# Doubling levels of a 64x64 triangular inverse: 32 of 64 columns a head instead of all

## The chip, the cores and the metric

The kernel runs on one core of one Trainium2 chip. The metric is the device time of one launch in microseconds (us). Before the change three runs gave 3709.69, 3712.32 and 3714.06 us, so the median is 3712.32 us. Lower is better. Engine names as in the profile: PE is the matmul engine (TensorE), PEld its weight loads, DVE the vector engine, ACT the scalar engine, POOL GpSimd, SP the queue that starts most transfers.

## The reference, cut to what matters

A model of four layers on 512 tokens of width 1024, in fp32: two layers of a first kind, then two of a second kind (`l` = 0 and 1 below). A layer of the second kind has three mixers side by side: an attention over picked keys (DSA), the RWKV-7 recurrence and the gated delta rule. The last two are recurrences over time with 4 heads of width 64 each. In chunks of 64 tokens the delta rule reads:

```python
lower = jnp.where(strict, jnp.einsum('bhncd,bhnsd->bhncs', kb, k) * decay, 0.0)
sol = lax.linalg.triangular_solve(jnp.eye(C) + lower, rhs,      # C = 64
                                  left_side=True, lower=True, unit_diagonal=True)
u, wk = sol[..., :Dv], sol[..., Dv:]
```

RWKV-7 is given as a step-by-step scan, and has a chunked form of the same kind. So for each chunk of 64 tokens and each of 8 heads a unit triangular 64x64 matrix has to be inverted or solved with. That inverse is the place of the change.

## The kernel before, in words

Each engine has its own program, and semaphores tie them together. The 512 tokens are four tiles of 128. A tile holds two chunks of 64 tokens: chunk 0 in partitions 0 to 63, chunk 1 in partitions 64 to 127. The function `rec_tile(l, j, stock)` stands once in the program of each of PE, DVE, ACT and POOL and handles tile `j` of layer `l` for both recurrences: 4 RWKV heads in columns 0 to 255 and 4 delta-rule heads in columns 256 to 511, 64 columns a head. It is a generator: each `yield` ends a step, and `tile_rounds` (L417) puts the steps of neighbouring tiles in turn, so that the instructions of tile `j`'s inverse stand in each engine's queue between the preparation of tile `j+1` and the end of tile `j-1`. The order on each engine is fixed by this at build time. Tile 0's preparation and most of its inverse lie in the rounds of the DSA attention (`mixer_rounds`, L370). The other three tiles come after it, with only the recurrence to do, and behind them the output projection begins.

The inverse is built by doubling. `Dm` starts as the identity plus level 0, `Dt` is its transpose, `N` the strictly triangular matrix (negated). Level k = 1 to 5 joins blocks of width 2^k into blocks of twice that:

- PE: `Y_k = N^T-product with Dm` (each head and chunk one 64x64 by 64x64 matmul), in two groups `g` of four heads, one PSUM bank a group, keys `("y", k, g)`. It waits for `Dm` of the level before.
- ACT (L3309): copies each group, 128x256, from the bank to `Yk` in SBUF. Key `("Y", k, g)`.
- PE: `d_k` from `Dt` and `Yk` into one bank of 512 columns; it waits for both copies and for `Dt` of the level before. For k < 5 also `dt_k` from `Yk` and `Dt`, the transposed product.
- DVE (L2617): copies `d_k` into `Dm` with a predicate, 128x512, where the mask of level k is 1; for k < 5 (L2623) the same for `dt_k` into `Dt`.

The masks `lvm(k, tr)` (L636) hold a 64x64 pattern that is broadcast over the heads: for `tr` = 0 it is 1 only in columns whose block of width 2^k has an odd number (and rows of the even block beside it), for `tr` = 1 only in columns of even blocks. All other columns are computed and never copied, or copied to `Yk` and used only for columns that no mask keeps.

The helper `each` (L1595 to L1601, its matmul L1600) issues 8 matmuls a group: 4 heads by 2 chunks, the two chunks in different halves of the array's rows and columns. In the trace a matmul of fp32 operands is two instructions. Per tile and layer that is 10 groups for Y, 10 for d, 8 for dt, 16 instructions each; for 4 tiles and 2 layers 3584 instructions, 80 copies on ACT, 40 on DVE at L2617 and 32 at L2623.

`keep_warm(b, n)` (L752) issues n matmuls of 384 columns whose result is not used. Before the change three such places stand in the recurrence (12 of them in tile 1, L1501, and 12 in tile 3 at level 1, L1609, and some between attention units). They stay as they are.

Of the kernel before, what the change touches and what calls it, by code (L numbers as in the profile page):

```python
# [9 lines left out]
I32 = mybir.dt.int32  # L10
# [5 lines left out]
P = 128  # L16
T = 512
NT = 4
D = 1024
# [424 lines left out]
def build_program(nc, A, out, dbg):  # L444
    ctx = ExitStack()
    with ctx:
# [54 lines left out]
        def bc(ap, shape):  # L501
            return ap.broadcast_to(shape)
# [7 lines left out]
        def h64(ap, n):  # L510
            return ap.rearrange("p (h d) -> p h d", h=n)
# [39 lines left out]
        rows, o = {}, 0  # L551
# [81 lines left out]
        def c64(n, k=1):  # L633
            return cr[:, R_X + n * 64:R_X + (n + k) * 64].bitcast(F32)

        def lvm(k, tr, n=4):  # L636
            return bc(c64(k + 6 * tr).unsqueeze(1), [P, n, 64])

        mc_bibs, mc_br, mc_id = c64(12, 2), c64(14), c64(15)
        HALF = (slice(0, 64), slice(64, 128))  # L640
# [81 lines left out]
        def tensor_program(pe):  # L722
# [26 lines left out]
            mm = partial(pe.matmul, skip_group_check=True)  # L749
            tr = partial(pe.transpose, identity=ident)  # L750
# [685 lines left out]
            def rec_tile(l, j, stock):  # L1436
# [8 lines left out]
                def S(*k):  # L1445
                    return pe.sig("rec", *k, l, j)
# [5 lines left out]
                for n, srcs in enumerate(([hbT[:, a, js] for a in range(4)],  # L1452
                                          [hbT[:, 4, js], hbT[:, 5, js], gT[:, 4, js], gT[:, 5, js]],
                                          [gT[:, a, js] for a in range(4)])):
                    b, free = bank(K("in", n), K("in", n))
                    pe.wait_ge(*free)
                    for m, s in enumerate(srcs):
                        ins = tr(b[:, m * P:(m + 1) * P], s)
# [8 lines left out]
                ins = mm(b1[:, 0:256], hbT[0:32, 6, js], lora[0:32, :], True, True)  # L1467
                if l:
                    pe.wait_ge(*at("rec", "vz", l))
                    ins = mm(b1[:, 256:512], vz[0:32, js], vup[0:32, :], True, True)  # L1470
# [18 lines left out]
                for p in range(4):  # L1489
                    ins = mm(b3[:, 256 + 2 * p:258 + 2 * p], LW[:, p * P:(p + 1) * P], ind, True, True)  # L1490
# [8 lines left out]
                b, free = bank(K("F4"), K("F4"), of=("rec", "od", l, j - 2) if j > 1 else None)  # L1499
# [3 lines left out]
                for a in range(2):  # L1503
                    tr(b[:, (2 * a + 0) * P:(2 * a + 1) * P], QK[:, a * P:(a + 1) * P])
                    ins = tr(b[:, (2 * a + 1) * P:(2 * a + 2) * P], KB[:, 256 + a * P:384 + a * P])
# [5 lines left out]
                b, free = bank(K("F3"), K("F3"), of=("rec", "o", 0, l, j - 2) if j > 1 else None)  # L1511
                pe.wait_ge(*free)
                pe.wait_ge(*at(*K("Qh")))
                for a in range(2):
                    tr(b[:, a * P:(a + 1) * P], QK[:, 256 + a * P:384 + a * P])
                    ins = tr(b[:, (2 + a) * P:(3 + a) * P], Qh[:, 256 + a * P:384 + a * P])
# [3 lines left out]
                b, free = bank(K("F1"), K("F1"))  # L1520
                pe.wait_ge(*free)
                pe.wait_ge(*at(*K("KBx")))
                for a in range(2):
                    tr(b[:, (2 * a) * P:(2 * a + 1) * P], Qh[:, a * P:(a + 1) * P])
                    ins = tr(b[:, (2 * a + 1) * P:(2 * a + 2) * P], KB[:, a * P:(a + 1) * P])
# [5 lines left out]
                b, free = bank(K("F2"), K("F2"))  # L1531
                pe.wait_ge(*free)
                pe.wait_ge(*at(*K("BT")))
                for a in range(4):
                    ins = tr(b[:, a * P:(a + 1) * P], BT[:, a * P:(a + 1) * P])
# [3 lines left out]
                b, free = bank(K("gd"), K("DN0"))  # L1539
                pe.wait_ge(*free)  # L1540
                pe.wait_ge(*at("rec", "gg", l))
                for h in range(4):
                    for c in HALF:
                        ins = mm(b[c, h * 64:(h + 1) * 64], bc(gg[c, j, h:h + 1], [64, 64]), m_bi[c, c], True, True)
# [4 lines left out]
                for par in range(2):  # L1549
                    if par:  # L1550
                        yield
                    b, free = bank(K("RW", par), K("RW", par))
# [4 lines left out]
                    for q in range(2):  # L1557
                        for n in range(2):
                            for e_, c in enumerate(HALF):
                                o = q * 256 + n * P  # L1560
                                ins = mm(b[c, o:o + P].rearrange("p (c n) -> p c n", c=2),
                                         F2[rs, n * 256 + q * P + 64 * e_:n * 256 + q * P + 64 * e_ + 64],
                                         f1v[rs, q, :, c], True, True)
                    ins.then_inc(*S("rw", par))
                yield
                N = get()
                for par in range(2):
                    b, free = bank(K("N", par), K("N", par))
# [4 lines left out]
                    for a, (lhs, rhs) in enumerate(((f1v, F2), (f4v, F3))):  # L1573
                        for q in range(2):
                            for e_, c in enumerate(HALF):
                                ins = mm(b[c, (2 * a + q) * 64:(2 * a + q + 1) * 64], lhs[rs, q, 1, c],
                                         rhs[rs, q * P + 64 * e_:q * P + 64 * e_ + 64], True, True)
                    ins.then_inc(*S("n", par))
                yield
                for par in range(2):  # L1580
                    b, free = bank(K("PN", par), K("PN", par))
                    pe.wait_ge(*free)
                    rs = HALF[par]
                    for q in range(2):
                        for e_, c in enumerate(HALF):
                            ins = mm(b[c, q * P:(q + 1) * P].rearrange("p (c n) -> p c n", c=2),
                                     F3[rs, q * P + 64 * e_:q * P + 64 * e_ + 64], f4v[rs, q, :, c], True, True)
# [3 lines left out]
                PN, Dm, Dt = get(), get(), get()  # L1591
                yield MADE
                stock.put(pe, l, DTN, F4)

                def each(b, g, lhs, rhs, o=0):  # L1595

                    for h in range(4):
                        for c in HALF:
                            hs = slice(g * 256 + h * 64, g * 256 + h * 64 + 64)
                            ins = mm(b[c, o + h * 64:o + (h + 1) * 64], lhs[c, hs], rhs[c, hs], True, True)  # L1600
                    return ins  # L1601

                yield
                for k in range(1, 6):
                    Yk = get()
                    for g in range(2):
                        b, free = bank(K("y", k, g), K("Y", k, g))
                        pe.wait_ge(*free)
                        keep_warm(b, 12 if j == 3 and k == 1 and not g else 0)  # L1609
                        pe.wait_ge(*at(*K("D", k - 1, g)))  # L1610
                        each(b, g, N, Dm).then_inc(*S("y", k, g))
                    if j == 3 and k == 4:
                        for q in ("dve", "act"):
                            pe.wait_ge(*at("dsa over", l, q))
                        to_T(("out", l), mx, lambda i, c: ("rec", "mixed", l, i), (0,))
                    yield
                    b, free = bank(K("d", k), K("D", k, 1), of=K("y", k, 0))
                    pe.wait_ge(*free)
                    pe.wait_ge(*at(*K("Dt", k - 1)))
                    for g in range(2):  # L1620
                        pe.wait_ge(*at(*K("Y", k, g)))
                        ins = each(b, g, Dt, Yk, 256 * g)
                    ins.then_inc(*S("d", k))
                    if k < 5:
                        b, free = bank(K("dt", k), K("Dt", k), of=K("y", k, 1))
                        pe.wait_ge(*free)
                        for g in range(2):
                            ins = each(b, g, Yk, Dt, 256 * g)
                        ins.then_inc(*S("dt", k))
                    if j == 3 and k == 4:  # L1630
                        to_T(("out", l), mx, lambda i, c: ("rec", "mixed", l, i), (1,))
                    stock.put(pe, l, Yk)
                    yield
# [3 lines left out]
                b, free = bank(K("x"), K("X"))  # L1637
# [4 lines left out]
                for h in range(4):  # L1642
                    o = (h // 2) * 256 + 192
                    for c in HALF:
                        ins = mm(b[c, h * 64:(h + 1) * 64], RW[h % 2][c, o:o + 64], VV[c, h * 64:(h + 1) * 64], True, True)
                ins.then_inc(*S("x"))
                for e_, c in enumerate(HALF):
                    b, free = bank(K("wt", e_), K("WT", e_))
# [10 lines left out]
                for par in range(2):  # L1659
# [4 lines left out]
                    for q in range(4):  # L1664
                        h = 2 * q + par
# [115 lines left out]
        def vector_program(v):  # L1781
# [19 lines left out]
            def psum_of(*key):  # L1801
                return psum[book.bank.get(key, 0)]
# [673 lines left out]
            def rec_tile(l, j, stock):  # L2476
                js = slice(j * P, (j + 1) * P)

                def K(*k):
                    return ("rec",) + k + (l, j)  # L2480

                def S(*k):
                    return v.sig("rec", *k, l, j)
# [126 lines left out]
                for k in range(1, 6):  # L2610
                    Yk = get()
                    if j == 3 and k == 5:
                        low(("out", l), 0)
                    yield
                    v.wait_ge(*at(*K("D", k - 1, 1)))
                    v.wait_ge(*at(*K("d", k)))
                    v.copy_predicated(h64(Dm, 8), lvm(k, 0, 8).bitcast(I32),  # L2617
                                      h64(psum_of(*K("d", k))[:, :], 8)).then_inc(*S("D", k, 1))
                    v.also(*K("D", k, 0))
                    if k < 5:  # L2620
                        v.wait_ge(*at(*K("Dt", k - 1)))
                        v.wait_ge(*at(*K("dt", k)))
                        v.copy_predicated(h64(Dt, 8), lvm(k, 1, 8).bitcast(I32),  # L2623
                                          h64(psum_of(*K("dt", k))[:, :], 8)).then_inc(*S("Dt", k))
                    stock.put(v, l, Yk)
                    if j == 3 and k == 5:
                        low(("out", l), 1)
                    yield
# [113 lines left out]
        def scalar_program(s):  # L2742
# [38 lines left out]
            def psum_of(*key):  # L2781
                return psum[book.bank.get(key, 0)]
# [427 lines left out]
            def rec_tile(l, j, stock):  # L3210
                def K(*k):
                    return ("rec",) + k + (l, j)

                def S(*k):
                    return s.sig("rec", *k, l, j)
# [89 lines left out]
                for k in range(1, 6):  # L3305
                    Yk = get()
                    for g in range(2):
                        s.wait_ge(*at(*K("y", k, g)))
                        copy(Yk[:, g * 256:g * 256 + 256], psum_of(*K("y", k, g))[:, 0:256]).then_inc(*S("Y", k, g))  # L3309
                    yield  # L3310
                    stock.put(s, l, Yk)
                    if j == 3 and k > 3:
                        high(("out", l), k - 4)
                    yield
# [479 lines left out]
```

## Time and profile before

| | |
|---|---|
| Median of 3 runs | 3712.32 us (3709.69 to 3714.06) |
| Profiled execution | span 3708.2 us; no other time of that execution is given |
| PE busy | 3610.1 us, 97% of the span, 23122 instructions |
| Weight loads (PEld) | 2996.1 us, 81% |
| DVE, ACT, POOL | 1972.4, 1502.7, 1623.7 us |
| Chain that ended last | PE 83%, DVE 10%, ACT 4% |

The busy time of PE is a union over pipelined matmuls: each matmul of 64 columns is recorded with 218 ns, while 64 of them follow each other within about 2 us. So the pace of PE is read from how many instructions fit in a stretch, not from the duration of one. The recurrence of layer l = 0 lies at about 1980 to 2125 us, that of l = 1 at about 3146 to 3296 us.

### The profile page before, as it was taken

To read this page: it belongs to the slowest core of one execution; us is meant where nothing else is said; L and a number is where in the kernel's file an instruction comes from. 1 tells how busy PE (TensorE), PEld (TensorE's weight loads), DVE (VectorE), ACT (ScalarE), POOL (GpSimd) and SP (SyncE) were. 2 spreads that over 40 slices of the span, in tenths; PEclk is the share of its full clock that TensorE was granted. 3 is DMA by queue.
4 is the path that set the end of the run, shared out by engine and by line. 5 is a ranking of instruction groups with operands and counts; after the bars stand their busy time and mean duration, and the time that the engine had idled before them with its cause. 6 is when DMAs were issued, how large, how long until landed. Compare 5 with 4: busy or idle time off the path is not lost.

```text
span 3708.2 us, 55795 instructions
## 1 busy us (share of the span) xinstructions
PE 3610.1 (97%) x23122; PEld 2996.1 (81%) x23122; DVE 1972.4 (53%) x3453; ACT 1502.7 (41%) x2665; POOL 1623.7 (44%) x883
## 2 busy tenths in 40 slices
PE   9999999999899999999999899999999999999999
PEld 8878888888788888888767888888888866788887
DVE  2356554344645544553677745544652496765552
ACT  3444333434433343333555443334333455534332
POOL 3114566421266635664322135664665322225664
PEclk9999999999999999999999999999999999999999
DMA  4103332311243234322210034323332220012332
GB/s 130 40 29 99 112 103 68 89 52 35 69 136 102 63 101 132 103 63 89 74 46 2 3 125 121 103 66 112 103 102 81 83 57 24 3 42 89 99 103 97
DMA packets 393405, 291.95 MB, mean 79 GB/s; under 512 B 17056, under 2 KB 355904, under 8 KB 393152
## 3 DMA queue, kind: packets, MB, share of 16 engines
q1 hardware_dynamic: 387728, 284.49, 25.2%
q10 hardware_dynamic: 5136, 2.70, 0.4%
q8 instruction: 183, 3.00, 0.3%
q0 software_dynamic: 288, 1.18, 0.1%
q14 instruction: 70, 0.57, 0.1%
HBM read 286.24 MB, written 2.10 MB: 78 GB/s over the span
## 4 chain that ended last, share of the span: by engine, by line
PE 83%; DVE 10%; ACT 4%; issue 1%; POOL 1%; ACTq 0%; DMA 0%; DVEq 0%; SPq 0%; POOLq 0%
PE ps L811 13%; PE ps L812 13%; PE ps L813 13%; PE ps L1040 4%; PE ps L1042 4%; PE ps L1041 4%; PE ps L943 3%; PE ps L940 3%; PE ps L942 3%; PE ps L1068 2%; PE ps L1600 2%; PE ps L1088 2%; PE ps L1077 1%; PE ps L1150 1%; PE ps L838 1%
## 5 line engine op out<-in xcount | busy, mean ns | idle before, releaser
L3453 POOL TENSOR_TENSOR wl<-wraw,wh 128x1024 fp32r<-128x1024 f32 (+1 forms) x424 | 1026.4, 2426 | 1553.1 <-ACT wh L2771 1549.6
L811 PE MATMUL ps<-x_T,wh 128*128 128x512 f32 (+1 forms) x2224 | 850.2, 382 | 0.0
L812 PE MATMUL ps<-x_T,wh 128*128 128x512 f32 (+1 forms) x2224 | 849.0, 382 | 0.0
L813 PE MATMUL ps<-x_T,wl 128*128 128x512 f32 (+1 forms) x2224 | 849.0, 382 | 0.0
L2771 ACT ACTIVATE wh<-wraw 128x1024 fp32r<-128x1024 f32 (+1 forms) x424 | 446.0, 1053 | 763.1 <-PE ps L813 489.1
L811 PEld LDWEIGHTS ps<-x_T,wh 128*128 128x128 f32 x2224 | 418.5, 188 | 81.1 <-issue 0.5
L813 PEld LDWEIGHTS ps<-x_T,wl 128*128 128x128 f32 x2224 | 418.4, 188 | 80.6
L812 PEld LDWEIGHTS ps<-x_T,wh 128*128 128x128 f32 x2224 | 418.4, 188 | 80.7 <-issue 0.5
L2048 DVE TENSOR_TENSOR scr<-scr,ps 128x512 f32<-128x512 f32 x132 | 90.7, 687 | 465.3 <-ACT scr L2926 465.3
L1040 PE MATMUL ps<-wh,h_T 128*128 128x512 f32 x672 | 262.5, 391 | 0.4
L1041 PE MATMUL ps<-wl,h_T 128*128 128x512 f32 x672 | 261.5, 389 | 0.0
L1042 PE MATMUL ps<-wh,h_T 128*128 128x512 f32 x672 | 261.5, 389 | 0.0
L3449 POOL TENSOR_TENSOR wl<-arena,wh 128x512 fp32r<-128x512 f32 x126 | 187.7, 1493 | 121.9 <-ACT wh L2768 121.8
L2094 DVE SCALAR_TENSOR_TENSOR x_tm<-ps,x_tm 128x512 f32<-128x512 f32 x224 | 155.0, 692 | 157.6 <-PE ps L943 78.3
L3449 POOL TENSOR_TENSOR wl<-mix,wh 128x512 fp32r<-128x512 f32 x150 | 212.6, 1433 | 8.2 <-ACT wh L2768 8.2
L2055 DVE TENSOR_TENSOR scr<-scr,ps 128x512 f32<-128x512 f32 x96 | 65.9, 686 | 217.4 <-PE ps L813 216.8
L1040 PEld LDWEIGHTS ps<-wh,h_T 128*128 128x128 f32 x672 | 126.1, 188 | 30.4 <-POOL wl L3449 2.7
L1042 PEld LDWEIGHTS ps<-wh,h_T 128*128 128x128 f32 x672 | 126.1, 188 | 26.3
L1041 PEld LDWEIGHTS ps<-wl,h_T 128*128 128x128 f32 x672 | 126.1, 188 | 25.8
L2768 ACT ACTIVATE wh<-mix 128x512 fp32r<-128x512 f32 x150 | 91.8, 624 | 125.3 <-PE ps L813 47.8
L940 PE MATMUL ps<-wh,h_T 128*128 128x512 f32 x352 | 138.0, 392 | 0.0
L943 PE MATMUL ps<-wh,h_T 128*128 128x512 f32 x352 | 137.1, 390 | 0.0
(816 smaller groups left out, 6877.6 us busy)
## 6 DMA issues: line engine op xcount, KB each, us to landing
wraw<-in_ffn_w_gate_dram SPq DMA_DIRECT2D x88, 512.0 KB, 3.9
wraw<-in_ffn_w_up_dram SPq DMA_DIRECT2D x88, 512.0 KB, 3.9
wraw<-in_w_in_dram SPq DMA_DIRECT2D x82, 512.0 KB, 3.8
wraw<-in_w_gate_dram SPq DMA_DIRECT2D x44, 512.0 KB, 3.9
wraw<-in_w_up_dram SPq DMA_DIRECT2D x44, 512.0 KB, 3.8
mix<-in_ffn_w_down_dram SPq DMA_DIRECT2D x20, 1024.0 KB, 7.1
arena<-in_ffn_w_down_dram SPq DMA_DIRECT2D x12, 1024.0 KB, 6.2
wraw<-in_ffn_w_down_dram SPq DMA_DIRECT2D x24, 512.0 KB, 3.7
```

Source lines behind the costliest of these rows:

```text
L811: mm(b[:, t0:t1], wh[:, k, :], xTh[:, k, t0:t1], k == 0, False)
L812: mm(b[:, t0:t1], wh[:, k, :], xTl[:, k, t0:t1], False, False)
L813: ins = mm(b[:, t0:t1], wl[:, k, :], xTh[:, k, t0:t1], False, k == 7)
L940: mm(o, lh(k, j), wh[:, q, :], k == 0, False)
L943: ins = mm(o, ll(k, j), wh[:, q, :], False, k == K - 1 and not apart)
L1040: mm(b[:, :], hF[:, q, 0, m, t], wh[:, u, :], first and q == 0, False)
L1041: mm(b[:, :], hF[:, q, 0, m, t], wl[:, u, :], False, False)
L1042: ins = mm(b[:, :], hF[:, q, 1, m, t], wh[:, u, :], False, q == pairs - 1)
L2094: return stt(xs, b[:, :], -0.5 if minus else 0.5, xs, ALU.mult, ALU.add)
L2771: copy(hl_of(w)[0], raw_of(w)).then_inc(*s.sig("w", "hi", w))
L3449: tt(wl[:, u, :], fast_src(prod, q), wh[:, u, :].bitcast(F32), ALU.subtract).then_inc(*g.sig("w", "lo", w, u))
L3453: tt(wl, raw_of(w), wh.bitcast(F32), ALU.subtract).then_inc(*g.sig("w", "lo", w))
```

## The change

The matmuls of levels 1 to 5 stream 32 of the 64 columns of their moving operand: the odd blocks of `Dm` for Y, the odd blocks of `Yk` for d, the even blocks of `Dt` for dt. The results lie side by side ("packed") in the bank, 32 columns a head: 128 columns a group, 256 for all. The stationary operand keeps its 64 columns, and the number of matmuls stays. ACT copies 128 packed columns a group into the odd blocks of `Yk` and leaves the even blocks with what the buffer held. DVE copies 256 packed columns with a predicate into the odd blocks of `Dm` (even blocks of `Dt`), with the mask cut to the same columns. Waits, keys, banks, buffers and the order of instructions on each engine stay.

```diff
+        def level(ap, k, odd):
+            return ap.rearrange("p (b s n) -> p b s n", s=2, n=2 ** k)[:, :, odd, :]
+        def packed(ap, k):
+            return ap.rearrange("p (b n) -> p b n", n=2 ** k)
+        def heads_of(ap, k):
+            return ap.rearrange("p (h b) n -> p h b n", h=8)
+        def level_mask(k, tr):
+            m = level(c64(k + 6 * tr), k, 1 - tr)
+            return bc(m.unsqueeze(1), [P, 8, 32 // 2 ** k, 2 ** k]).bitcast(I32)
...
-                            ins = mm(b[c, o + h * 64:o + (h + 1) * 64], lhs[c, hs], rhs[c, hs], True, True)
+                            ins = mm(packed(b[c, o + h * 32:o + (h + 1) * 32], k), lhs[c, hs], level(rhs[c, hs], k, odd),
+                                     True, True)
...
-                        each(b, g, N, Dm).then_inc(*S("y", k, g))
+                        each(b, g, k, N, Dm, 1).then_inc(*S("y", k, g))
...
-                        ins = each(b, g, Dt, Yk, 256 * g)
+                        ins = each(b, g, k, Dt, Yk, 1, 128 * g)
...
-                            ins = each(b, g, Yk, Dt, 256 * g)
+                            ins = each(b, g, k, Yk, Dt, 0, 128 * g)
...
-                    v.copy_predicated(h64(Dm, 8), lvm(k, 0, 8).bitcast(I32),
-                                      h64(psum_of(*K("d", k))[:, :], 8)).then_inc(*S("D", k, 1))
+                    v.copy_predicated(heads_of(level(Dm, k, 1), k), level_mask(k, 0),
+                                      heads_of(packed(psum_of(*K("d", k))[:, 0:256], k), k)).then_inc(*S("D", k, 1))
...
-                        v.copy_predicated(h64(Dt, 8), lvm(k, 1, 8).bitcast(I32),
-                                          h64(psum_of(*K("dt", k))[:, :], 8)).then_inc(*S("Dt", k))
+                        v.copy_predicated(heads_of(level(Dt, k, 0), k), level_mask(k, 1),
+                                          heads_of(packed(psum_of(*K("dt", k))[:, 0:256], k), k)).then_inc(*S("Dt", k))
...
-                        copy(Yk[:, g * 256:g * 256 + 256], psum_of(*K("y", k, g))[:, 0:256]).then_inc(*S("Y", k, g))
+                        copy(level(Yk[:, g * 256:g * 256 + 256], k, 1),
+                             packed(psum_of(*K("y", k, g))[:, 0:128], k)).then_inc(*S("Y", k, g))
```

## Rows read from the trace of the kernel before

**Rows 1.** The page: the chain that ended last, shares of the span by engine.

```profile
PE 83%; DVE 10%; ACT 4%; issue 1%; POOL 1%; ACTq 0%; DMA 0%; DVEq 0%; SPq 0%; POOLq 0%
```

**Rows 2.** Ten windows that cover both recurrences: sum of lengths, busy us by engine.

```profile
sum 295.00, PE 266.97 PEld 235.97 DVE 225.21 ACT 136.70 POOL 57.67; mean PE 26.70 PEld 23.60 DVE 22.52 ACT 13.67 POOL 5.77
```

**Rows 3.** The same ten windows, L1600 alone.

```profile
sum 295.00, PE 128.98 PEld 118.01; mean PE 12.90 PEld 11.80
```

**Rows 4.** Chain of waits, layer 0, tile 1 in order: start, us, what.

```profile
2027.82 0.73 DVE arena L2623
...
2044.22 0.74 DVE scr L2617
...
2054.84 0.59 issue
```

**Rows 5.** Chain of waits, layer 1, tiles 0, 1 and 3.

```profile
3172.26 0.64 DVE spare L2617
...
3213.10 0.58 issue
...
3283.89 0.74 DVE wraw L2617
```

**Rows 6.** Groups by form on DVE and ACT: busy, mean ns.

```profile
L2617 DVE COPY_PREDICATED scr<-cr,ps 128x512 f32<-128x512 int32 x5 | 3.7, 736 | 1.2 <-PE ps L1600 1.2
...
L2607 DVE COPY_PREDICATED scr<-cr,spare 128x256 f32<-128x256 int32 x1 | 0.4, 443 | 0.0
...
L3179 ACT ACTIVATE scr<-ps 128x256 f32<-128x256 f32 x8 | 3.1, 384 | 7.3 <-PE ps L1077 7.2
...
L3179 ACT ACTIVATE scr<-ps 128x384 f32<-128x384 f32 x5 | 2.5, 491 | 1.9 <-PE ps L1077 1.8
```

**Rows 7.** Timeline of PE, runs of equal matmuls: start, us, form, idle before.

```profile
2035.16 0.95 PE L1490 MATMUL ps<-con,spare 128*128 128x2 f32 x8
...
2055.19 0.60 PE L1586 MATMUL ps<-scr 64*64 64x128 f32 x12
2055.73 1.53 PE L1458 MATMUL ps<-cr,arena 128*128 128x128 f32 x12
...
3219.11 1.08 PE L1600 MATMUL ps<-scr,spare 64*64 64x64 f32 x29 [0.17 <-DVE scr L2617]
```

**Rows 8.** Timeline of PE around a fall of the clock in the first layer.

```profile
720.57 2.73 PE L1334 MATMUL ps<-con,arena 128*128 128x1 f32 x24
...
724.58 0.63 PE L813 MATMUL ps<-x_T,wl 128*128 128x512 f32 x1
```

**Rows 9.** Windows: length, busy PE, PEld, DVE, ACT, POOL, granted clock, DMA.

```profile
724.10:727.50 3.40, 3.40 (x9) 2.65 (x9) 0.36 (x4) 2.16 (x2) 1.15 (x1) 0.51 0.21 72
...
2038.00:2042.00 4.00, 3.99 (x132) 3.79 (x126) 3.76 (x9) 3.31 (x12) 0.00 (x0) 1.00 0.02 4
2042.00:2045.00 3.00, 0.94 (x7) 0.50 (x5) 2.86 (x9) 0.74 (x2) 1.97 (x2) 1.00 0.00 0
2045.10:2048.10 3.00, 3.00 (x38) 2.55 (x39) 2.93 (x5) 1.26 (x3) 2.64 (x3) 0.50 0.00 0
...
3213.30:3216.50 3.20, 2.55 (x64) 2.29 (x66) 3.13 (x5) 1.85 (x4) 2.84 (x3) 1.00 0.02 5
...
3229.60:3232.90 3.30, 3.30 (x43) 2.65 (x43) 1.42 (x4) 0.38 (x1) 0.00 (x0) 0.50 0.01 2
```

**Rows 10.** Chain of waits: the same work at either clock, layer 1 tiles 1 and 2.

```profile
3192.09 1.01 PE ps L1667 x29
3194.14 1.63 PE ps L1600 x56
...
3230.80 1.79 PE ps L1667 x29
3234.46 2.53 PE ps L1600 x56
```

**Rows 11.** Share of L1600 in the chain of waits of layer 0's recurrence.

```profile
by line: PE ps L1600 28.2%; issue 4.8%; PE ps L1686 2.8%; PE ps L1667 2.3%; PE ps L1561 1.8%; PE ps L1088 1.7%; POOL small L3495 1.6%; PE ps L1484 1.5%; DVE small L2664 1.5%; PE ps L1696 1.5%; PE ps L781 1.5%; DVE spare L2579 1.4%; PE ps L1
```

More of the change, by code:

```diff
@@ L1593, in rec_tile, with each @@
                 stock.put(pe, l, DTN, F4)
-                def each(b, g, lhs, rhs, o=0):
+                def each(b, g, k, lhs, rhs, odd, o=0):
                     for h in range(4):
```

## The prediction

> **What bounds the kernel.** I read the page's chain first: PE holds 83% of it, DVE 10% [rows 1]. Outside the two recurrences nothing changes, so I went on to windows over those stretches. They are 295 us long in all; PE is busy for 267.0 of them, DVE for 225.2, ACT for 136.7 [rows 2]. The changed matmuls (L1600) make up 129.0 us of PE's busy time, and their weight loads are busy for 118.0 [rows 3]. So neither engine sets the pace alone: the chain changes between them several times a tile. The reader should look in it for two things: copies at L2617 and L2623 that stand on it, and stretches of L1600. In layer 0's recurrence L1600 holds 28.2% of the chain [rows 11].
>
> **Part 1: the copies.** Today a predicated copy of 512 columns takes 736 ns, one of 256 columns 443 ns [rows 6]: -0.29 us a copy. There are 72 of them (40 at L2617, 32 at L2623), so DVE loses 21 us of work. Most of that stands beside other work. On the chain of layer 0 I count for tile 1: L2623 at 2027.82 (DVE goes on to L2645, for which PE waits), L2617 at 2044.22 (PE waits for it), and L2617 before the "issue" piece at 2054.84, where DVE can begin its next product only after the copy [rows 4]. Tile 2 repeats the pattern, tile 3 has two (after its wait for tile 2's end, and at level 5). That is 8, or -2.3 us. Layer 1: two in tile 0 (3172.26 and the L2623 behind it), then in tiles 1 and 2 the same three, L2623 at 3213.10 in addition, and one at level 4 of which only 0.17 us can be had, since PE waits no longer than that [rows 5, 7]; two in tile 3 (the first at 3283.89) [rows 5]. That is 2 + 2 x 4 + 2 = 12, plus 2 x 0.17: -3.8 us. ACT's copies shrink by 0.11 us each (384 ns for 256 columns, 491 for 384, so half of 256 saves 491 - 384 = 107) [rows 6]; 80 copies make 8.6 us, nearly all beside PE; about two are on the path: -0.2 us. Sum of part 1: -6.3 us.
>
> No row shows a copy whose pieces are only 2 elements long with gaps of 2, as at level 1. Bounds: 0 if the gaps eat the saving everywhere, -0.29 as taken; the same count of copies with 0 saved gives 0. Below, if DVE were the pace for all 21 us and ACT hidden: -21. I take -6.3, since the packed side and most levels have long pieces.
>
> **Part 2: what PE's instructions cost.** The number stays (3584), the weights stay 64 columns, the streamed columns halve. What paces a matmul, weights or streamed columns? With weights of 128 columns, 8 matmuls of 2 columns take 0.95 us and 12 of 128 columns take 1.53 us; take off the last one's tail (0.2) and it is 0.11 and 0.12 us each, for 64 times the columns [rows 7]. So there the weight load sets the pace. With weights of 64 columns, 29 L1600 take 1.08 us, 0.031 each, and 12 L1586 with 128 columns take 0.54 us from their start to that of the next group, 0.045 each [rows 7]. If the columns entered linearly, 32 fewer would save (0.045 - 0.031)/2 = 0.007 us each, 25 us in all, about half of it on the path (28.2% of the 140 us of layer 0 are 39.5 [rows 11], and L1600 has half of its 129 us [rows 3] there). Bounds: 0 and -13 us. I take 0, because of the 2-column row. PE's reads of `Dm` and `Yk` now have gaps; a read even twice as slow would fit under the load, so I take 0 here too.
>
> **Part 3: the clock.** This is where I expect the change to cost. PE runs at 2.4 GHz except in some stretches, and in the first layer one fall comes with no idle at all: 24 matmuls of one column, back to back for 2.73 us, and soon after them 512-column matmuls of 0.63 us [rows 8] at a granted clock of 0.51, that is 1.2 GHz [rows 9]. PE was full of instructions, but streamed almost nothing. In the recurrence: a window dense with L1600 (132 matmuls in 4 us) runs at 1.00; 3 us in which PE did only 7 transposes are followed by 0.50 [rows 9]; and the start of tile 2's levels in layer 1 (from 3229.60), after a wait of PE and one group of L1600, runs at 0.50 too [rows 9]. Against it: the same transposes before 3213.30 in layer 1 were followed by 1.00 [rows 9]. So the recurrence already runs near the point where the clock falls, and the change takes half the streamed columns out of its commonest matmul. It also makes it harder to come back: after a fall, the matmuls that should lift the clock stream half as much.
>
> Price: L1667 x29 takes 1.79 us at the lower clock and 1.01 at the full one, L1600 x56 2.53 (the last of it at full clock) and 1.63 [rows 10]. So 1.68 us are lost in 4.32, or 0.39 us for each us at 1.2 GHz. Today 13.5 us of the recurrences run there (two stretches of 3.4 in layer 0, one of 6.7 in layer 1, found by moving such windows along; [rows 9] show a part of one of each kind): 5.3 us paid already. Places a layer where thin work meets L1600: tile 0's levels between attention units; the first level of tiles 1 and 2 (as at 3227); the transposes amid tiles 1 and 2, and the wait in tile 3. I count five a layer, the two first levels as one, ten in all, and leave out one, in layer 1, where DVE sets the pace (L2623 at 3213.10 on the chain [rows 5]) and would hide it. Nine falls of 6.8 us (as the one from 3229.60) at 0.39 are 23.9 us; less the 5.3 paid today: +18.6. This is the least certain term: bounds 0 (the clock doesn't see the difference) and half of the 295 us at the lower clock, 57.5 - 5.3 = +52.
>
> The Trainium skill, "TensorE: Matmul & The Clock Gate", section "Why this matters for your kernels", says that drops mid-kernel come from long idle gaps of PE between bursts. By that rule the changed levels, still dense, would keep the clock, and the sum would be that of rival 1 below. The trace disagrees at 720.57, where there was no gap [rows 8].
>
> **Sum.** -6.3 + 0 + 18.6 = +12.3 us. The profiled execution has a span of 3708.2 us, 4.1 below the median of the runs, 3712.3; I apply the difference to the median: 3724.6 us (+0.33%).
>
> **Rivals.**
> 1. The clock stays as it is, the copies pay. For it: no tile's L1600 run fell by itself, and the 3213.30 row. Against it: rows 8. Time: 3712.3 - 6.3 = 3706.
> 2. The other side, by PE: columns set part of L1600's pace. Then -13 - 6.3 = -19, 3693. For it: L1586's 0.045 against 0.031; against it the 2-column row. It decides if a 32-column matmul follows the last within 0.027 us instead of 0.031.
> 3. A few more falls: three of 6.8 us beyond those paid, 8.0 - 6.3 = +2, 3714.
> 4. The change doesn't save what it says: the gapped copies take as long as before, with the falls: +18.6, 3731; without them, 3712.
>
> **Chances.** Forecast 0.46, rival 1 0.28, rival 3 0.13, rival 2 0.07, rival 4 0.06. A difference under 0.2% (7.4 us) can't be told from none here. Rival 1 lies just inside of it, and I give it a third of its chance beyond: with rival 2, faster is 0.17. Same: the rest of rival 1, rival 3 and a part of the forecast, 0.36. Slower: 0.47. Range: from rival 1, a little below, 3704, to 3750, where +44 of part 3's upper bound of +52 would be reached.
>
> **What would show it.** L2617 and L2623 at about 440 ns, L3309 at about 280 (part 1); L1600 still at 0.031 us each at full clock (part 2); a granted clock under 1.00 in far more of 1980 to 2125 and 3146 to 3296 us, above all in tile 0's levels and in tile 3 (part 3). I am wrong if those windows show the same 13.5 us at 0.50 as today, or if L1600's pace at full clock falls under 0.028 us.

## The result, and the profile after

The changed kernel takes 3762.0 us (median of 4 runs, 3760.12 to 3767.52) against 3711.0 us of the kernel before (4 runs, 3707.47 to 3714.06): ratio 1.0136, 95% interval 1.0124 to 1.0148. It is 51 us slower. The forecast was 3724.6 us with a range to 3750; the direction was right, the size four times too small.

In what follows a thin matmul is one that streams 32 columns. In the diffs and rows below, L1615 is the matmul that was L1600, L2633 and L2639 are the predicated copies that were L2617 and L2623, and L3325 is ACT's copy that was L3309.

The page after: the 40 slices of PE and of the clock it was granted, and the chain by engine, which answers to [rows 1].

```profile
span 3761.5 us, 55795 instructions
...
PE   9999999999999999999999999999999999999999
...
PEclk9999999999999999999997799999999998879999
...
PE 85%; DVE 9%; ACT 4%; issue 1%; POOL 1%; DMA 0%; ACTq 0%; DVEq 0%; SPq 0%; POOLq 0%
```

All slices are full of PE work, and the clock digit falls in slices 22, 23 and 34 to 36: the two recurrences. Before, every digit of that line was 9. The other engines are busy for no longer than before (DVE 1958.8 us against 1972.4, ACT 1495.6 against 1502.7).

The recurrences as windows, from the first level matmul to the last copy, first of the kernel before, then after (columns as in [rows 9]: length, busy us of PE, PEld, DVE, ACT, POOL, granted clock).

```profile
1984.00:2121.00 137.00, 125.90 (x3008) 112.04 (x3008) 104.37 (x232) 64.11 (x157) 28.93 (x24) 0.98 0.01 3
3150.00:3292.00 142.00, 127.83 (x3014) 113.72 (x3014) 108.89 (x240) 64.35 (x157) 28.75 (x24) 0.98 0.01 3
```

```profile
1985.00:2146.00 161.00, 151.97 (x3008) 137.74 (x3008) 98.28 (x232) 60.98 (x158) 28.72 (x24) 0.78 0.01 3
3179.60:3344.00 164.40, 154.25 (x3014) 140.06 (x3014) 102.10 (x240) 61.42 (x157) 28.57 (x24) 0.77 0.01 2
1986.00:2010.00 24.00, 24.00 (x308) 21.63 (x304) 5.37 (x19) 6.38 (x22) 0.00 (x0) 0.51 0.01 2
2054.30:2074.80 20.50, 19.96 (x280) 18.44 (x280) 13.85 (x30) 7.01 (x14) 5.69 (x5) 0.51 0.01 2
2098.70:2115.80 17.10, 16.66 (x272) 15.62 (x272) 10.70 (x21) 4.55 (x11) 4.86 (x5) 0.51 0.01 2
2136.20:2149.90 13.70, 13.16 (x195) 12.18 (x194) 7.80 (x17) 3.88 (x9) 0.00 (x0) 0.51 0.01 1
3180.70:3204.60 23.90, 23.90 (x299) 21.52 (x297) 5.05 (x17) 6.54 (x23) 0.00 (x0) 0.50 0.01 1
3252.40:3269.50 17.10, 16.24 (x250) 15.08 (x247) 10.58 (x21) 5.97 (x13) 3.44 (x3) 0.51 0.01 2
3293.40:3313.90 20.50, 19.76 (x317) 18.51 (x318) 13.83 (x29) 5.63 (x14) 5.89 (x5) 0.50 0.01 2
3330.90:3348.00 17.10, 16.11 (x228) 15.07 (x229) 8.74 (x19) 4.43 (x11) 1.64 (x1) 0.51 0.01 2
```

The same instructions fill 325.4 us instead of 279.0: 46.4 of the 53.3 us between the two spans. PE is busy for 306.2 us instead of 253.7, DVE and ACT for less. The lower eight rows are the stretches at 1.2 GHz, found by moving windows along: four a layer, one for each tile, 13.7 to 24 us long, 154 us in sum. Before there were short ones ([rows 9] show a part of two). In the first of them PE was busy for 24.00 of 24.00 us: nothing waited there, it had only gone slow. All eight begin beside a short pause of PE: 0.63 us ahead of tile 0's levels, 1.65 to 1.69 us amid the transposes of tiles 1 and 2, 1.29 us in tile 3. The kernel before has such pauses at the same places (0.64 us at 1983.96, for one, and no fall behind it), so the pauses alone are not the cause.

The same place in tile 0 of layer 0 on PE's timeline (start, us, form), before and then after:

```profile
1986.86 2.08 PE L1600 MATMUL ps<-spare 64*64 64x64 f32 x64
1988.87 0.66 PE L1088 MATMUL ps<-arena,scr 128*128 128x64 f32 x4
...
1994.17 3.25 PE L1600 MATMUL ps<-spare 64*64 64x64 f32 x96
1997.35 1.53 PE L1458 MATMUL ps<-cr,arena 128*128 128x128 f32 x12
```

```profile
1989.08 3.62 PE L1615 MATMUL ps<-spare 64*64 64x32 f32 x64
1992.64 1.11 PE L1103 MATMUL ps<-arena,scr 128*128 128x64 f32 x4
...
2002.03 5.33 PE L1615 MATMUL ps<-spare 64*64 64x32 f32 x96
2007.29 2.82 PE L1473 MATMUL ps<-cr,arena 128*128 128x128 f32 x12
...
2011.33 0.89 PE L1615 MATMUL ps<-spare 64*64 64x32 f32 x24
```

64 matmuls of half the columns take 3.62 us instead of 2.08. Neighbours that the change doesn't touch slow down with them (L1088, now L1103: 0.66 to 1.11). The full pace is back only behind L1473, twelve matmuls of 128 columns: then 24 of L1615 take 0.89 us. That these wider matmuls lifted the clock is not shown: in the run with tile 0 alone thin, below, they did not.

### The profile page after: what moved, and what is told of

It reads as the page before. It is cut to its first block, busy times and chain, and to the rows that moved or that the text cites. A ratio compares the mean times of both kernels' runs of the same rounds, so it can differ in the third digit from the quotient of the medians.

```text
span 3761.5 us, 55795 instructions
## 1 busy us (share of the span) xinstructions
PE 3670.7 (98%) x23122; PEld 3055.8 (81%) x23122; DVE 1958.8 (52%) x3453; ACT 1495.6 (40%) x2665; POOL 1622.7 (43%) x883
## 4 chain that ended last, share of the span: by engine, by line
PE 85%; DVE 9%; ACT 4%; issue 1%; POOL 1%; DMA 0%; ACTq 0%; DVEq 0%; SPq 0%; POOLq 0%
PE ps L826 13%; PE ps L828 13%; PE ps L827 13%; PE ps L1055 4%; PE ps L1056 4%; PE ps L1057 4%; PE ps L1615 3%; PE ps L958 3%; PE ps L955 3%; PE ps L957 3%; PE ps L1083 2%; PE ps L1103 2%; PE ps L1092 1%; PE ps L1165 1%; PE ps L853 1%
```

## The experiments

Theory: the thinner matmuls make the clock fall in the recurrences and then do not lift it. Rivals: the gapped or packed addresses of the copies or of PE's reads and writes cost the time; or a wait that the new copies bring.

**PE streams all 64 columns, the copies stay short**, from their places in the bank:

```diff
-  ins = mm(packed(b[c, o + h * 32:o + (h + 1) * 32], k), lhs[c, hs], level(rhs[c, hs], k, odd), True, True)
+  ins = mm(b[c, 2 * o + h * 64:2 * o + (h + 1) * 64], lhs[c, hs], rhs[c, hs], True, True)
...
-  heads_of(packed(psum_of(*K("d", k))[:, 0:256], k), k)      # dt and ACT's y likewise
+  heads_of(level(psum_of(*K("d", k)), k, 1), k)
```

> PE streams all 64 columns as before; only the copies on ACT and DVE take the 32 kept columns of each head, straight from their places in the bank. Theory (the clock falls because half as many columns are streamed): the granted clock in both recurrences is as before, about 17 us at 1.2 GHz, and the shorter copies are all that is left: 20 copies on the path at 0.23 us (the 500 ns that the changed kernel shows against 733) and a little of ACT, -5 us against before, 3706. Rival A (the shorter copies move the order of waits and so bring the clock down): 3750 or more. Rival B (gapped reads of the bank cost as much as they save): 3711.

Measured: 3706.9 us against 3713.3, ratio 0.9986 (0.9977 to 0.9995). The windows of its recurrences:

```profile
1986.50:2121.00 134.50, 122.63 (x3008) 109.73 (x3008) 97.62 (x233) 59.77 (x157) 28.72 (x24) 1.00 0.01 3
3150.00:3289.00 139.00, 126.58 (x3014) 113.17 (x3014) 102.19 (x243) 60.67 (x158) 28.57 (x24) 0.98 0.01 3
```

The short copies alone are a small gain (273.5 us for the recurrences, 5.5 under the kernel before), so the loss of the changed kernel must come with the halved matmul. Rival A is out.

**All 64 columns streamed, but in gapped order, kept blocks first**, so that PE reads `Dm`, `Dt` and `Yk` with gaps and the bank holds the kept columns packed:

```diff
-  ins = mm(b[c, 2 * o + h * 64:2 * o + (h + 1) * 64], lhs[c, hs], rhs[c, hs], True, True)
+  ins = mm(halves(b[c, 2 * o + h * 64:2 * o + (h + 1) * 64], k), lhs[c, hs], both(rhs[c, hs], k, odd), True, True)
+  # both: blocks "p (b s n) -> p s b n", the kept s first; halves: "p (s b n) -> p s b n"
```

> PE streams 64 columns a matmul, but in another order: first the 32 kept ones in the same pieces with gaps as in the changed kernel, then the other 32; the copies read the first 32 of each head. Theory (number of columns): clock as before, time as with all 64 in plain order, about 3706. Rival C (the gaps in what PE reads bring the clock down or slow PE, not the number of columns): as the changed kernel, 3750 to 3762.

Measured: 3707.1 us, 0.9983 (0.9974 to 0.9992), the same as the one above. Gaps in PE's operand cost nothing that can be measured here, and the copy gains nothing from a packed source. Only the number of columns streamed is left.

**PE halved, copies whole, nothing packed:**

```diff
+  ins = mm(level(b[c, 2 * o + h * 64:2 * o + (h + 1) * 64], k, odd), lhs[c, hs], level(rhs[c, hs], k, odd), True, True)
   # the copies of the kernel before; what they copy beside the kept columns is not used
```

> PE streams the 32 columns only and writes them to their places in the bank; ACT and DVE copy all 64 columns as before (the other 32 of the bank are what it held, and no mask keeps them). Theory (columns): the falls of the clock stay, the saving of the copies goes: the changed kernel plus 5 us, 3767; about 160 us of both recurrences at 1.2 GHz. Rival A (copies are the cause): 3711.

Measured: 3773.8 us, 1.0160 (1.0146 to 1.0174). Its windows:

```profile
1986.00:2151.00 165.00, 155.67 (x3008) 140.40 (x3008) 105.03 (x232) 64.83 (x157) 28.91 (x24) 0.76 0.01 3
3184.00:3352.00 168.00, 160.50 (x3014) 144.95 (x3014) 109.13 (x240) 65.73 (x157) 28.74 (x24) 0.74 0.01 2
```

The halved matmul by itself is the slowdown, and more than all of it: 60.5 us. Against the kernel before, nothing differs but which columns PE streams.

**The same in tile 0 alone, and in tiles 1 to 3 alone** (`if j == 0`, or `if j > 0`, ahead of the halved `mm`):

> As the run with half stream and full copies, but only in tile 0 of each layer; the other three tiles stream 64 columns. Theory (columns, locally): the long stretch at 1.2 GHz in tile 0's levels, 23.9 us in the changed kernel, comes back in both layers, and the others (tiles 1 to 3) stay as before: 2 x 24 us at 0.39 us lost a us, +19 us at most, 3725; less if tile 0's stretch also moves where later falls land. Rival D (one fall starts the next, so that later tiles fall too): 3740 or more.

> The complement of the run with half stream in tile 0 only: tile 0 streams 64 columns, tiles 1 to 3 the kept 32, copies as before. If each tile's levels bring their own fall, the two parts add up to the run with half stream everywhere (+60.5 us): +60.5 - 23.6 = +37, 3750. If falls chain from tile to tile (rival D), the parts add up to more than the whole: 3755 or over.

Measured: tile 0 alone 3736.9 us, 1.0061 (1.0048 to 1.0075), that is 23.6 us; tiles 1 to 3 alone 3755.4 us, 1.0111 (1.0092 to 1.0129), 41.8 us. Together 65 us, and all tiles at once cost 60.5. Both runs came out above their forecasts (3725 at most, and 3750), and the second lies on the line drawn for rival D, 3755. The sum alone doesn't decide: it is 5 us over the whole, and the two intervals reach 5 and 7 us to either side. The windows do. First those of the run with tile 0 alone thin, two for each layer:

```profile
1986.00:2023.60 37.60, 37.60 (x435) 31.58 (x434) 13.68 (x36) 14.46 (x37) 3.67 (x3) 0.50 0.01 2
2023.60:2137.00 113.40, 103.86 (x2575) 94.20 (x2574) 90.70 (x197) 50.09 (x120) 25.06 (x22) 0.97 0.01 3
3169.00:3194.40 25.40, 25.15 (x328) 22.77 (x329) 7.61 (x21) 7.45 (x23) 0.00 (x0) 0.53 0.00 1
3194.40:3321.70 127.30, 116.64 (x2690) 103.42 (x2686) 101.58 (x221) 57.54 (x135) 28.72 (x24) 0.93 0.01 3
```

Then tile 0's levels, and the first stretch of tile 1, in the run with tiles 1 to 3 thin:

```profile
1986.00:2010.00 24.00, 22.41 (x398) 18.81 (x392) 15.00 (x32) 13.85 (x36) 6.59 (x6) 1.00 0.01 3
2040.70:2057.80 17.10, 17.10 (x267) 15.98 (x265) 11.19 (x21) 6.29 (x12) 3.67 (x4) 0.51 0.01 2
```

A long stretch at 1.2 GHz comes in the tiles that are thin and in no other: tile 0 with 64 columns keeps 1.00, and tile 1 falls though tile 0 had not. So none is only the late return from an earlier fall. Where tile 0 alone is thin, only short falls come behind its stretch: two of 3.4 us in layer 0, as in the kernel before, and 17 us in three pieces in layer 1, where the kernel before has one of 6.7.

The length is less orderly. In layer 1 tile 0's stretch is 24 us in both kernels, but in layer 0 it lasts 37.6 us here against 24 with all tiles thin, though the same work stands in it. PE's timeline of this run:

```profile
2008.44 2.82 PE L1473 MATMUL ps<-cr,arena 128*128 128x128 f32 x12
2018.75 2.07 PE L1499 MATMUL ps<-arena,con 128*128 128x512 f32 x2
```

The twelve matmuls of 128 columns behind which the changed kernel had its full pace back stand here at the same place, run at 1.2 GHz too (2.82 us in both), and the clock stayed down for 12 us more, through four matmuls of 512 columns. What ends a stretch is not shown by these runs.

**Half of the heads thin**, heads 0 and 2 with 32 columns, 1 and 3 with 64, short copies:

```diff
+  if h % 2 == 0:
+      ins = mm(level(b[...], k, odd), lhs[c, hs], level(rhs[c, hs], k, odd), True, True)
+  else:
+      ins = mm(b[...], lhs[c, hs], rhs[c, hs], True, True)
```

> Full-stream kernel with the short copies, but of the four heads of a group the first and third stream their 32 kept columns and the others all 64: 48 on average. Theory (columns): between 3707 (all 64) and 3762 (all 32) with a granted clock between theirs; if the time at 1.2 GHz grows evenly with the columns left out, some 90 us of both recurrences and 3734. If the fall is a matter of crossing a point, far from the middle: under 3715 or over 3750. Rival A or C (something else than the columns): no ordering between the three is forced.

Measured: 3717.2 us, 1.0018 (1.0006 to 1.0031), with runs from 3710 to 3729 us. Its profile is of one near the upper end (span 3727.5): clock 0.95 in layer 0 and 0.86 in layer 1.

```profile
1991.00:2131.00 140.00, 128.33 (x3008) 114.81 (x3008) 98.31 (x234) 60.24 (x157) 28.74 (x24) 0.95 0.01 3
3157.50:3311.40 153.90, 142.84 (x3014) 127.78 (x3014) 101.83 (x240) 60.66 (x157) 28.59 (x24) 0.86 0.01 3
```

The loss goes with how thin the stream is, but not in proportion: halfway in columns is 10 us above all 64 (3706.9) and 45 under all 32 (3762.0), and varies from run to run. It lies between the two outcomes that were named, 3734 for an even growth and under 3715 for a point that is crossed, so the form of the dependence stays open.

**The changed kernel with more work for PE**: two matmuls of 384 columns, of which nobody uses the result, ahead of the first Y group and ahead of d of each level (156 in all).

```diff
-                        keep_warm(b, 12 if j == 3 and k == 1 and not g else 0)
+                        keep_warm(b, 12 if j == 3 and k == 1 and not g else 0 if g else 2)
...
                     pe.wait_ge(*free)
+                    keep_warm(b, 2)
                     pe.wait_ge(*at(*K("Dt", k - 1)))
```

> The changed kernel, with work added: before the first group of Y and before d of each level two matmuls of 128 rows and 384 columns whose result is not used, 160 in all and 0.17 to 0.2 us each (27 to 32 us of PE, some of it inside PE's waits). Theory (the clock answers to streamed columns): the long falls go, 57 us come back, 10 to 30 are paid: 3715 to 3735, faster than the changed kernel although it does more. Rival (the clock falls for another cause in the changed matmuls): the falls stay and the time rises to 3780 or more.

Measured: 3734.8 us, 1.0066 (1.0041 to 1.0091) of the kernel before, and so 27 us less than the changed kernel, which does less work. The runs range from 3729 to 3753 us; these windows are of one that took 3730.5:

```profile
1987.00:2134.00 147.00, 143.21 (x3085) 122.13 (x3084) 97.92 (x232) 60.36 (x157) 28.75 (x24) 1.00 0.01 3
3164.50:3313.00 148.50, 144.31 (x3090) 123.18 (x3090) 101.86 (x240) 61.00 (x157) 28.61 (x24) 1.00 0.01 3
```

The group of those wide matmuls, 294 before and 450 here (busy us, mean ns):

```profile
L770 PE MATMUL ps<-cr 128*128 128x384 f32 x450 | 107.1, 362 | 0.9 <-DVE small L2565 0.9
```

And the same place in tile 0 of layer 0 as above, on PE's timeline:

```profile
1989.99 0.62 PE L770 MATMUL ps<-cr 128*128 128x384 f32 x2
1990.54 2.06 PE L1615 MATMUL ps<-spare 64*64 64x32 f32 x64
1992.53 0.66 PE L1103 MATMUL ps<-arena,scr 128*128 128x64 f32 x4
```

With them the clock stays at 1.00, and 64 thin matmuls take 2.06 us: what 64 of 64 columns took (2.08). That takes the fall away and leaves the change in place. The added matmuls also fill pauses of PE (the one of 0.63 us ahead of tile 0's levels is gone), so this run by itself doesn't tell columns from pauses; the runs above do, with the same pauses and 64 columns. The recurrences last 295.5 us, 29.9 less than in the changed kernel. They are 22.0 above the kernel that streams all 64 columns, which is what the added matmuls cost: too much to be worth it.

**The form of the copy.** The new predicated copies average 491 to 503 ns, not 443 as forecast. By level, in tile 1 of the changed kernel (DVE's timeline, levels 1 and 2):

```profile
2037.94 0.73 DVE L2633 COPY_PREDICATED scr<-cr,ps 128x256 f32<-128x256 int32 x1 [0.26 <-PE ps L1615]
2038.88 0.73 DVE L2639 COPY_PREDICATED arena<-cr,ps 128x256 f32<-128x256 int32 x1 [0.20 <-PE ps L1615]
2043.06 0.43 DVE L2633 COPY_PREDICATED scr<-cr,ps 128x256 f32<-128x256 int32 x1 [0.17 <-PE ps L1615]
```

At level 1, where the kept runs are 2 elements long, the copy of 256 columns takes as long as one of 512 did [rows 6]. Which operand does it? The kernel before, with 32 instructions on 256 columns added at the end of DVE's program (the small helpers that form the patterns are left out; the comments give the line and the operands):

```diff
+ for _ in range(4):                                                                            # line, dst / mask / src
+     step(v.copy_predicated(h8(gap(dst, 2)), m8(gap(mk, 2)), h8(row(src[:, 0:256], 2))))        # 2755 gaps / gaps / packed
+     step(v.copy_predicated(h8(gap(dst, 2)), m8(row(mk[:, 0:32], 2)), h8(row(src[:, 0:256], 2)))) # 2756 gaps / packed / packed
+     step(v.copy_predicated(h8(row(dst[:, 0:256], 2)), m8(gap(mk, 2)), h8(row(src[:, 0:256], 2)))) # 2757 packed / gaps / packed
+     step(v.copy_predicated(h8(row(dst[:, 0:256], 2)), m8(row(mk[:, 0:32], 2)), h8(gap(src, 2)))) # 2758 packed / packed / gaps
+     step(v.copy_predicated(h8(gap(dst, 4)), m8(gap(mk, 4)), h8(row(src[:, 0:256], 4))))        # 2759 runs of 4
+     step(v.copy_predicated(h8(row(dst[:, 0:256], 2)), m8(row(mk[:, 0:32], 2)), h8(row(src[:, 0:256], 2)))) # 2760 packed
+     step(v.tensor_copy(gap(dst, 2), row(src[:, 0:256], 2)))                                    # 2761
+     step(v.tensor_copy(dst[:, 0:256], src[:, 0:256]))                                          # 2762
```

> The kernel before, with 32 instructions added at the end of VectorE's program (four rounds of eight, each of 256 columns, one waiting for the last); what they write is read by nobody. In this order: (1) a predicated copy whose destination and mask are runs of 2 elements with gaps of 2, from a packed source; (2) destination with gaps, mask packed; (3) destination packed, mask with gaps; (4) source with gaps, the other two packed; (5) destination and mask in runs of 4 with gaps of 4; (6) all packed; (7) a plain copy into runs of 2 with gaps; (8) a plain packed copy. The question is which operand makes the level-1 copy of 256 columns take 730 ns where those of levels 2 to 5 take 427 to 444. [...] Rival A: the mask's short runs: (1), (3) near 730, (2) near 430. Rival B: either alone is enough: (1), (2), (3) near 730. Rival C: it is the number of runs in any operand, the source's too: (4) also near 730. If (1) itself is near 430 here, the form of the copy is not the cause at all. Of the time of the whole kernel I expect 15 to 25 us more (32 instructions of 0.4 to 0.75 us), if VectorE ends near the kernel's end.

Measured, groups by form (busy us, mean ns of one):

```profile
L2755 DVE COPY_PREDICATED scr<-cr,ps 128x256 f32<-128x256 int32 x4 | 2.9, 722 | 0.1
L2756 DVE COPY_PREDICATED scr<-cr,ps 128x256 f32<-128x256 int32 x4 | 2.9, 722 | 0.1
L2758 DVE COPY_PREDICATED scr<-cr,ps 128x256 f32<-128x256 int32 x4 | 1.8, 440 | 0.1
L2757 DVE COPY_PREDICATED scr<-cr,ps 128x256 f32<-128x256 int32 x4 | 1.8, 440 | 0.1
L2760 DVE COPY_PREDICATED scr<-cr,ps 128x256 f32<-128x256 int32 x4 | 1.8, 440 | 0.1
L2759 DVE COPY_PREDICATED scr<-cr,ps 128x256 f32<-128x256 int32 x4 | 1.7, 425 | 0.1
L2761 DVE COPY scr<-ps 128x256 f32<-128x256 f32 x4 | 1.7, 425 | 0.1
L2762 DVE COPY scr<-ps 128x256 f32<-128x256 f32 x4 | 1.7, 424 | 0.1
```

It is the destination alone: 722 ns with gaps of 2 in it, 440 with gaps in the mask or the source only, 425 with runs of 4. A plain copy into the same gapped destination takes 425, no more than the packed one (that it would take more was expected, and wrong). What is slow is a predicated copy into runs of 2 elements. The kernel as a whole took 3729.2 us against 3708.1 in its one run, 21 more; its added instructions stand behind each other from 3709.66 to the end.

## Why the prediction was wrong in size

**Part 1, the copies: right in kind, and less than forecast.** The bound of gaps that eat the saving was true at level 1 only: the saving is 0.31 us at levels 2 to 5 and 0 at level 1, 0.24 on average instead of 0.29. ACT's term was right: 384 less 107 was forecast, and it takes 277 ns.

```profile
L3325 ACT ACTIVATE spare<-ps 128x128 f32<-128x128 f32 x36 | 9.8, 277 | 48.0 <-PE ps L1615 47.8
```

The kernel with short copies alone shows the sum: -5.5 us in its recurrences and a ratio of 0.9986, -5.2 us with an interval of -8.5 to -1.9, against -6.3. A part of that is the clock too: layer 0 shows 1.00 there against 0.98 before, so the copies' own share is below 5.5. An estimate: its recurrences have 6.8 us at 1.2 GHz where those of the kernel before have 13.5, and 6.7 us less at the price of 0.37 found below are 2.5 of the 5.5. That leaves about 3 us for the copies, half of the 6.3 forecast; one profile of each kernel is little to rest it on.

**Part 2, PE's pace: right.** At full clock the chain after has

```profile
3274.37 1.01 PE ps L1683 x29
3276.42 1.61 PE ps L1615 x56
```

against 1.63 for 56 of L1600 in [rows 10], beside 29 of the untouched L1667 (now L1683) at 1.01 in both. At 1.2 GHz it is the same: 32 thin matmuls take 1.92 us (at 1994.11 in the changed kernel), 32 of all 64 columns 1.97 (at 2045.09 in the kernel before). Half the columns save nothing. That it is the weights which set the pace was argued from [rows 7]; no run changes them alone. The condition given for rival 2, 0.027 us, doesn't fit its term either: 0.007 us less than 0.031 would be 0.024.

**Part 3, the clock: the mechanism was right, the term mis-sized.** The step that failed is "Nine falls of 6.8 us ... at 0.39". The price held: from the kernel with short copies to the changed one the recurrences grow from 273.5 to 325.4 us, 51.9. The stretches are 154 us in sum; 7.9 of them lie behind the two windows, and the former kernel still has 6.8, so it is for 139 us, 0.37 us for each. The count held roughly: eight stretches instead of nine, at the places that were named, save the first levels of tiles 1 and 2. The length did not: 13.7 to 24 us, 19 on average, where 6.8 was assumed. I took the length from 3229.60, a fall in the kernel before, where the levels behind it still streamed 64 columns. The prediction itself had said that the matmuls which should lift the clock would stream half as much, and then gave that no price. In the changed kernel the levels did not lift it; it stayed down through 256 of L1615 in tile 0 of layer 0, 64, 32, 64 and 96 with attention products between. Why a stretch ends after 14 us in one tile and after 24 in another stays open, as said for the run with tile 0 alone. With 19 in place of 6.8, the prediction's own sum is 8 x 19 x 0.39 = 59 less 5.3 paid and less 6.3 for part 1: +48, against 51 measured. The stated upper bound, half of the 295 us, was about what came, and a chance beyond +44 should have been kept inside the range.

Outside the recurrences' windows the changed kernel's span is 6.9 us longer: 4.6 of it between the two recurrences (1033.6 us against 1029.0) with PE's busy time longer by 6.0, the rest ahead of and behind them. Part of it is the clock too: the 7.9 us of the last stretches, 3.9 of them in that gap. A stretch of 6.8 us at 3153.6, also in the gap, has none beside it in the kernel before, but the kernels with 64 streamed columns show one there as well and are not slower, so it can't be laid to the change.

**The rule on gaps.** The prediction set a fall with no gap at 720.57 against the rule on idle gaps in "TensorE: Matmul & The Clock Gate" of the Trainium skill, section "Why this matters for your kernels". The first stretch of the changed kernel decides: PE busy for 24.00 of 24.00 us at 0.51, and ahead of it a pause of 0.63 us, as long as the one at the same place in the kernel before (0.64 us), where the clock stayed at 1.00. By the rule the time would have been that of rival 1, 3706.

**Rivals.** 1 (the clock stays, 3706) is what the two kernels with 64 streamed columns gave, 3706.9 and 3707.1: its price was right, its condition was not met. 3 (a few falls) is met by none at 32 columns; half of the heads thin comes near it, 3717. 4 (gapped copies take as long as before) is true at level 1 alone, 16 of the 72 copies. 2 is refuted above.

## What to carry to other kernels

Before you cut the columns of small matmuls, ask what their pace is: if the columns don't set it (here 64 matmuls take 2.06 us with 32 columns and 2.08 with 64), the cut saves nothing, and here it held PE at 1.2 instead of 2.4 GHz for 154 us, where 13.5 were before. Don't take the length of a fall from the trace of before when the change thins the work behind it (here 6.8 us became 14 to 24). Take the part of such a change that pays by itself: here the short copies with full matmuls, 3707 us, are faster than the kernel before by 0.14% (0.05 to 0.23), about the least that can be measured here, and than the changed kernel by 1.5%.

## What was not expected of the hardware

- PE can run at 1.2 GHz for 24 us without a gap: work that was mostly dense matmuls of 64x64 weights and 32 columns went on at 0.51, while the same stretch with 64 columns ran at 1.00. Wider matmuls behind it don't always end it: with tile 0 alone thin it went on through twelve of 128 columns and lasted 37.6 us.
- Adding 156 matmuls of 384 columns (107.1 us busy in that group, 59.6 in the changed kernel's) made the kernel 27 us faster.
- A predicated copy of 256 fp32 columns takes 722 ns into runs of 2 elements, 425 into runs of 4, 440 packed; gaps in its mask or source cost nothing (440). The Trainium skill, "SBUF — State Buffer", section "Door 1: The DMA port swizzle (why `[64,N]` ≈ `[32,N]`)", speaks of lines of 16 bytes in SBUF and full bandwidth from two hits a line. Two elements of fp32 are two hits, and the plain copy agrees (425 against 424); the predicated one doesn't. Why, no run shows.
